# A decoder layer on one core: the first stage in another order

## The chip, the cores and the metric

The kernel runs on 1 core of a Trainium2 chip (trn2). The metric is device microseconds (us) of one execution; lower is better. The engines are PE (TensorE, matrix products), DVE (VectorE), ACT (ScalarE), POOL (GpSimd) and SP (SyncE, which only issues DMAs here). Each has its own instruction queue and runs it in order; they meet through semaphores.

## What is computed

One layer of a decoder with 1024 tokens of width 1024, all in fp32. The change touches only what happens before the attention rounds, so the reference is cut to that:

```python
n = _rmsnorm(h, g_mix[l])
proj = n @ w_in[l]
qa, ka, va, qb, kb, vb, gate_a, gate_b = jnp.split(proj, split_at, axis=-1)
qa = _partial_rope(heads(qa, N_HEADS_DIL), positions)
ka = _partial_rope(heads(ka, N_HEADS_DIL), positions)
o_a = merge(_dilated_attention(qa, ka, heads(va, N_HEADS_DIL)))
o_b = merge(_stick_breaking(heads(qb, N_HEADS_SB), heads(kb, N_HEADS_SB), heads(vb, N_HEADS_SB)))
...
h = h + _memory_attention(_rmsnorm(h, g_mem_q[l]), _rmsnorm(mem, g_mem_kv[l]), w_q_mem[l], w_kv_mem[l], w_o_mem[l])
```

The memory (256 tokens) has a norm of its own, and its keys and values are `_rmsnorm(mem) @ w_kv_mem`: four key heads and four value heads of 128. They are needed late, in the memory attention; the query, key and value of the first pair of A-heads are needed at once.

## The kernel before

**Tiles and passes.** Activations lie with the features on the 128 partitions, as eight blocks of 128 features by 1024 tokens. Every fp32 product is made of three products of rounded parts: `hi*hi`, `lo*hi` and `hi*lo`, where `hi` is the rounded number and `lo` the rest. A weight tile of 128 x 1024 is split into `w_hi` and `w_lo` by POOL (`split`, L455 for `w_hi` in two instructions, L460 for `w_lo` in four). There are two buffers of each, used in turn: POOL may start to split tile n when PE has begun tile n-1 (semaphore `w_begun`), and PE may begin tile n when it is split (`w_split`, `begin_tile`). SP loads the tiles in the order in which `weight_stream` has packed them. One tile of `w_in` against all tokens is 48 matmuls with 512 columns (two halves of three passes of eight); a tile of the memory's weights is 24 matmuls with 256 columns.

**The first stage.** The program begins with the eight tiles of the memory's weights, K0 to K3 (one key head each) and V0 to V3 (in pairs, each pair makes two blocks of the values), and then three tiles of `w_in`: QA, KA, VA, the query, key and value of the first pair of A-heads. On their way PE also makes the mean of the memory's squares (L570), turns the memory's norm factor into a column (L576), and makes the mean of x's squares (L583). ACT rounds x into `n_hi` (L979) and squares it (L983), block by block in turn; DVE makes the rest `n_lo` (L1468) and adds up the squares in `rms` (L1473). The norm of x isn't applied to `n_hi`: it multiplies the product when DVE reads it out of PSUM (`read_out`, L1506). The memory's keys go PE -> DVE (`k_f`, L1454) -> ACT (`km_out` hi, L962) -> DVE (`km_out` lo, L1457), the values PE -> ACT (L967) -> DVE (L1462); both are then stored to HBM by four DMAs that ACT issues (L1003, L1004).

**Rotation.** DVE makes the angles from the positions (L1436 to L1444, then L1485 to L1487), ACT their sine and cosine (L994, L996, with a table load ahead and one behind). When QA is read out, ACT issues four small DMAs that swap rows of it (`swap_dma`, L1011); DVE multiplies and adds (`rope`, L1520 to L1524), ACT rounds (L1016), DVE makes the rest (`lo_part`, L1513). Then the same for KA. VA is transposed by PE (L624) and rounded by ACT (L1020) and DVE (L1529).

**What follows.** Four rounds (`round_`, three in a loop and the last by itself), in which PE puts attention of one pair of heads between the passes of the next ten tiles (KB first); then the gated mix, the output product, memory attention, the feed-forward part and the last norm.

**Buffers.** The tensors of a stage lie in the same SBUF space as those of the stages before and after (`phase`); a store or a tile of the next stage may be written only when what lay there has been used. The eight PSUM banks are `ps[:, 0..7, :]`.

Of the kernel before, what the change touches and what calls it, by code (L numbers as in the profile page):

```python
# [17 lines left out]
ALU = mybir.AluOpType  # L18
ACT = mybir.ActivationFunctionType
# [147 lines left out]
HEAD_UNITS = 2 * HEAD_TILES  # L167

# [5 lines left out]
def build(nc, xT, memT, positions, gains, weights, ident_d, rope_d, bias_d, mask_d, outT):  # L174
    with ExitStack() as ctx:
# [26 lines left out]
        def phase(*tensors):  # L202
# [122 lines left out]
        gained = sem("gained")  # L325


        B_MIX = 2
# [37 lines left out]
        KEYS_AT = (4, 5, 7)  # L366
# [155 lines left out]
        def _(pe):  # L522
# [40 lines left out]
            pe.wait_ge(mg_lo_s, KT)  # L563
            for t in range(2 * MH):
                begin_tile(t + 1)
                if t == 1:
                    pe.wait_ge(msq, 1)
                    pe.wait_ge(summed, 1)
                    for k in range(KT):
                        ins = pe.matmul(ps[:, 7, 0:NM], mean_w[:], mem_sq[:, k, :], start=(k == 0), stop=(k == KT - 1))  # L570
                    ins.then_inc(mmean, 1)
                if t == MH:
                    pe.wait_ge(mrms, 1)
                    pe.wait_ge(ident_in, 16)
                    for mt in range(2):
                        ins = pe.transpose(ps[:, 1, blk(mt)], mem_r[:, blk(mt)], ident[:])  # L576
                    ins.then_inc(r_col_full, 1)
                if t == MH + 2:
                    pe.wait_ge(r_col_ready, 1)
                    pe.wait_ge(kv_lo_s, 2)  # L580
                    pe.wait_ge(summed, KT + 1)
                    for half in range(2):
                        pe.matmul(ps[:, half, :], mean_w[:], rms[:, blk(half, HALF)], start=True, stop=True  # L583
                                  ).then_inc(bank_full, 1)
                if t < MH:
                    lead, last = passes(ps[:, 2 + t, 0:NM], lambda k: (t % 2, k * P), lambda k: mg_hi[:, k, :],
                                        lambda k: mg_lo[:, k, :], (0, 1, 2), range(KT), True, True)
                    last.then_inc(kv_full, 1)
                else:
                    first = t % 2 == 0  # L590
                    for mt in range(2):
                        item = MH + (t - MH) // 2 * 2 + mt
                        n = 0
                        for a, w in ((mg_hi, w_hi), (mg_lo, w_hi), (mg_hi, w_lo)):
                            for k in range(KT // 2):
                                last = pe.matmul(ps[:, 2 + item % 6, 0:NM], a[:, k + (0 if first else KT // 2), blk(mt)],  # L596
                                                 w[:, t % 2, blk(k, NM)], start=(first and n == 0),
                                                 stop=(not first and n == 3 * KT // 2 - 1))
                                if mt == 0 and n == 0:
                                    lead = last  # L600
                                n += 1
# [3 lines left out]

            pe.wait_ge(nlo_ready, KT)

# [107 lines left out]
            for half in range(2):  # L715
                if half:
                    pe.wait_ge(vt_lo_s, half)
# [1344 lines left out]
```

## Time and profile before

| what | value |
|---|---|
| median of 3 runs | 1856.89 us (1855.19 to 1857.27) |
| profiled execution, its time | 1855.3 us |
| its span (first to last instruction) | 1853.3 us |
| PE busy in the span | 1729.2 us, 93% |
| DVE, ACT, POOL busy | 62%, 42%, 42% |
| chain that ended last, PE's share | 80% |
| mean granted TensorE clock | 0.972 |

The page cuts the span into 40 slices of 46.3 us; PE's digits there are 3, 7 and then mostly 9. "Busy" is the share of time in which an instruction of the engine ran; "idle before <- X" is how long the engine had nothing to run before a group of instructions, and which engine's instruction ended that wait.

### The profile page before, as it was taken

The numbers are of one execution on the slowest core, as the hardware profiler recorded it, in microseconds if no ns is written. First come the engines' busy times: TensorE is split into PE (matmuls) and PEld (weight loads), VectorE is DVE, ScalarE is ACT, GpSimd is POOL, SyncE is SP. The second block draws the span as 40 slices with busy tenths as digits, with TensorE's granted clock in tenths as the row PEclk, the third lists the DMA queues.
The fourth block names the chain that finished last, engine by engine and source line by source line (L and its number), as shares of the span: only waits on it lengthen the run. The fifth ranks groups of instructions, "written<-read, shape, count | busy, mean of one in ns | idle before, by whom it ended". The sixth has DMA issues, their size and how long they took to land.

```text
span 1853.3 us, 24985 instructions
## 1 busy us (share of the span) xinstructions
PE 1729.2 (93%) x8350; PEld 1398.7 (75%) x8350; DVE 1155.9 (62%) x1685; ACT 782.4 (42%) x1291; POOL 776.4 (42%) x894
## 2 busy tenths in 40 slices
PE   3799999999999999969999888999999999999996
PEld 3677777777777777758887766788888888788884
DVE  7446795689468846975444569745545445566667
ACT  4215773577358646753212334533433334200013
POOL 5733222232223221224454105665666656534445
PEclk8899999999999999979999889999999999999998
DMA  5311112101211211164212000131121221422222
GB/s 196 125 40 44 42 50 67 46 29 60 67 36 39 66 53 39 52 230 157 109 45 91 23 12 23 46 111 70 68 91 68 92 89 68 154 96 91 91 91 91
DMA packets 51711, 141.73 MB, mean 76 GB/s; under 512 B 6192, under 2 KB 14640, under 8 KB 51504
## 3 DMA queue, kind: packets, MB, share of 16 engines
q1 hardware_dynamic: 32256, 101.35, 15.6%
q10 hardware_dynamic: 19376, 39.33, 6.5%
q8 instruction: 48, 0.79, 0.2%
q14 instruction: 31, 0.25, 0.0%
HBM read 109.20 MB, written 30.41 MB: 75 GB/s over the span
## 4 chain that ended last, share of the span: by engine, by line
PE 80%; DVE 8%; issue 4%; ACT 3%; POOL 2%; DVEq 0%; ACTq 0%; DMA 0%; POOLq 0%
PE ps L537 46%; PE ps L856 21%; PE ps L683 4%; PE ps L646 3%; PE ps L660 3%; POOL w_lo L488 1%; DVE e_row L1599 1%; DVE pt L1629 1%; DVE e_row L1596 1%; DVE rows L1608 1%; PE ps L679 1%; DVE sum_a L1805 1%; DVE h L1962 0%; DVE n_lo L1811 0%; PE ps L596 0%
## 5 line engine op out<-in xcount | busy, mean ns | idle before, releaser
L455 POOL TENSOR_SCALAR w_hi<-w_stage 128x512 fp32r<-128x512 f32 x186 | 126.8, 700 | 868.2 <-issue 459.8
L460 POOL TENSOR_TENSOR w_lo<-w_stage,w_hi 128x256 fp32r<-128x256 f32 x372 | 342.9, 953 | 7.7
L537 PE MATMUL ps<-n_hi,w_hi 128*128 128x512 f32 x1184 | 329.4, 400 | 11.8 <-DVE n_lo L1549 7.0
L537 PE MATMUL ps<-n_lo,w_hi 128*128 128x512 f32 x1184 | 320.8, 392 | 0.0
L537 PE MATMUL ps<-n_hi,w_lo 128*128 128x512 f32 x1184 | 320.7, 392 | 0.0
L537 PEld LDWEIGHTS ps<-n_hi,w_hi 128*128 128x128 f32 x1184 | 222.1, 191 | 60.3 <-issue 12.0
L537 PEld LDWEIGHTS ps<-n_lo,w_hi 128*128 128x128 f32 x1184 | 220.8, 188 | 45.7 <-issue 0.2
L537 PEld LDWEIGHTS ps<-n_hi,w_lo 128*128 128x128 f32 x1184 | 219.9, 188 | 44.8
L488 POOL TENSOR_TENSOR w_lo<-w_stage,w_hi 128x256 fp32r<-128x256 f32 x176 | 164.7, 956 | 120.9 <-ACT w_hi L1259 120.9
L1699 DVE TENSOR_TENSOR h<-ps,h 128x512 f32<-128x512 f32 (+1 forms) x176 | 121.2, 690 | 123.3 <-PE ps L537 123.3
L1081 ACT ACTIVATE pt<-ps 128x256 fp32r<-128x256 f32 (+3 forms) x96 | 78.0, 813 | 133.9 <-PE ps L660 133.7
L1312 ACT ACTIVATE snap<-ps 128x512 f32<-128x512 f32 x88 | 52.6, 598 | 180.1 <-PE ps L856 180.0
L488 POOL TENSOR_TENSOR w_lo<-t_raw,w_hi 128x256 fp32r<-128x256 f32 x132 | 109.1, 847 | 43.7 <-ACT w_hi L1259 43.4
L1629 DVE TENSOR_TENSOR pt<-ps,pt 128x256 fp32r<-128x256 f32 (+3 forms) x96 | 91.9, 957 | 49.9 <-ACT pt L1081 45.9
L856 PE MATMUL ps<-left,w_hi 128*128 128x512 f32 x308 | 122.7, 398 | 0.0
L856 PE MATMUL ps<-n_hi,w_hi 128*128 128x512 f32 x352 | 115.5, 399 | 6.1 <-POOL w_lo L488 4.2
L856 PE MATMUL ps<-n_lo,w_hi 128*128 128x512 f32 x352 | 114.8, 397 | 2.6 <-DVE n_lo L1814 2.6
L856 PE MATMUL ps<-n_hi,w_lo 128*128 128x512 f32 x352 | 114.4, 396 | 0.0
L1506 DVE TENSOR_TENSOR raw<-ps,rms 128x512 f32<-128x512 f32 x80 | 54.8, 685 | 90.6 <-PE ps L537 90.6
L1364 ACT ACTIVATE n_hi<-n_lo 128x1024 fp32r<-128x1024 f32 x22 | 22.1, 1052 | 186.3 <-DMA n_lo<-hidden_scratch 186.3
L856 PEld LDWEIGHTS ps<-n_hi,w_hi 128*128 128x128 f32 x352 | 66.5, 190 | 23.9 <-POOL w_lo L488 5.1
L660 PE MATMUL ps<-ident,rows 128*128 128x128 f32 x576 | 81.8, 280 | 0.0
(236 smaller groups left out, 3027.3 us busy)
## 6 DMA issues: line engine op xcount, KB each, us to landing
w_stage<-weights_in SPq DMA_DIRECT2D x116, 512.0 KB, 3.4
w_stage<-weights_in SPq DMA_DIRECT2D x44, 256.0 KB, 2.6
hidden_scratch<-u_f SPq DMA_DIRECT2D x22, 512.0 KB, 5.7
n_lo<-hidden_scratch SPq DMA_DIRECT2D x22, 512.0 KB, 4.1
gates_scratch<-raw ACTq DMA_DIRECT2D x16, 512.0 KB, 2.8
o_scratch<-o_sum ACTq DMA_DIRECT2D x64, 64.0 KB, 2.1
n_lo<-o_scratch ACTq DMA_DIRECT2D x8, 512.0 KB, 3.9
g_a<-gates_scratch ACTq DMA_DIRECT2D x8, 512.0 KB, 3.7
```

Of the source, the lines that this page charges most:

```text
L455: ins = pool.tensor_scalar(w_hi[:, b, at], stage[:, b, at], 1.0, 1.0, ALU.mult, ALU.mult)
L460: ins = pool.tensor_tensor(w_lo[:, b, at], stage[:, b, at], w_hi[:, b, at].bitcast(F32), ALU.subtract)
L488: ins = pool.tensor_tensor(w_lo[:, b, at], right(name)[:, blk(part, 2 * P)], w_hi[:, b, at].bitcast(F32), ALU.subtract)
L537: ins = pe.matmul(bank, w[:, b, c:c + P], mv(k), start=(first and n == 0), stop=(last and n == total - 1))
L646: ins = pe.matmul(ps[:, 2 + h, 0:width(s)], a[hs, blk(qb)], b[hs, at], start=(n == 0), stop=(n == 2 and not diagonal))
L660: ins = pe.transpose(ps_t[:, h, n, :], rows[:, s % 4, h, blk(n)], ident[:])
L683: ins = pe.matmul(ps[:, r, blk(h, 2 * P)], v_of[m][:, c + kb, h, :, :].rearrange("p a d -> p (a d)"), pt[:, h, kb, :, :].rearrange("p a q ...
L856: ins = pe.matmul(ps[:, bank, :], w[:, b, c + k * P:c + (k + 1) * P], left(name, k)[p == 1], start=(opening and p == 0 and k == 0), stop=( ...
L1081: act.activation(pt[:, :, 0:n, 0, :], ps_t[:, :, 0:n, :], ACT.Copy).then_inc(pt_hi_s, 1)
L1506: dve.tensor_tensor(raw[:, RAW[name], blk(half, HALF)], ps[:, half, :], rms[:, blk(half, HALF)], ALU.mult).then_inc(bank_free, 1)
L1629: dve.tensor_tensor(pt[:, :, 0:n, 1, :], ps_t[:, :, 0:n, :], pt[:, :, 0:n, 0, :].bitcast(F32), ALU.subtract).then_inc(pt_lo_s, 1)
L1699: dve.tensor_tensor(hj, ps[:, bank + half, :], hj, ALU.add).then_inc(bank_free, 1)
```

## The change

The order of the first stage's tiles becomes K0, QA, K1, KA, K2, K3, V0, V1, V2, VA, V3 (`HEAD`); PE, the weight stream and the PSUM banks follow it. `memory_tile` and `head_tile` are the old loops, taken apart. The mean of the memory's squares no longer waits for the second tile; the mean of x's squares stands behind QA, in banks 6 and 7.

```diff
+HEAD = ("K0", "QA", "K1", "KA", "K2", "K3", "V0", "V1", "V2", "VA", "V3")
+HEAD_BANK = {"QA": 0, "KA": 2, "VA": 0}
+KV_BANK = (4, 5, 4, 5, 2, 3, 6, 7)
...
+                    if n >= 2:
+                        pe.wait_ge(kv_lo_s, n - 1)
...
+                    if n == 0:
+                        pe.wait_ge(bank_free, B_MIX + 4)
+                    if n == 2:
+                        pe.wait_ge(r_col_ready, 1)
...
+                    if name == "VA":
+                        pe.wait_ge(bank_free, B_MIX + half + 1)
...
+            memory_tile("K0")
+            pe.wait_ge(msq, 1)
+            pe.wait_ge(summed, 1)
+            for k in range(KT):
+                ins = pe.matmul(ps[:, 7, 0:NM], mean_w[:], mem_sq[:, k, :], start=(k == 0), stop=(k == KT - 1))
+            ins.then_inc(mmean, 1)
+            head_tile("QA", (0, 2, 1), ((nhi_ready, KT - 1), (nlo_ready, KT - 1)))
             pe.wait_ge(nlo_ready, KT)
+            pe.wait_ge(summed, KT + 1)
+            pe.wait_ge(mrms_raw, 1)
...
-            pe.wait_ge(kv_lo_s, 2 * MH)
+            pe.wait_ge(kv_lo_s, MH)
+            pe.wait_ge(bank_free, B_MIX + 6)
             for half in range(2):
-                if half:
-                    pe.wait_ge(vt_lo_s, half)
-                pe.wait_ge(bank_free, B_MIX + 6)
-                v_transposes(half, 5)
+                v_transposes(half, 4 + half)
+            pe.wait_ge(kv_lo_s, MH + 2)
```

On ACT all eight blocks of x are rounded first and then squared, and the norm factor (L955, L956) is made at once behind the squares. The four stores of the memory's keys and values move behind the rounding of VA, and the wait for them into the round:

```diff
                 act.activation(n_hi[:, k, :], x_f[:, k, :], ACT.Copy, scale=gain[:, G_MIX + k:G_MIX + k + 1]
                                ).then_inc(nhi_ready, 1)
+            for k in range(KT):
                 if k >= 2:
                     act.wait_ge(summed, k)
                 act.activation(sq0[:, k % 2, :], x_f[:, k, :], ACT.Square).then_inc(squared, 1)
...
+            kv_hi(0)
+            for n, name in enumerate(("QA", "KA")):
+                act.wait_ge(bank_free, B_MIX + 2 * n + 2)
+                swap_dma(n, n)
+                kv_hi(1 + n)
+                act.wait_ge(rope_done, n + 1)
+                round_hi(name)
+            for t in range(3, 2 * MH):
                 kv_hi(t)
...
-            act.wait_ge(kv_out, 64)
...
+                    if s == N_A - 2:
+                        act.wait_ge(kv_out, 64)
```

On DVE the eight rests of x come ahead of the sums; the first sum adds two squares and the clearing of `rms` goes; two of the three steps that reduce the angles, and what follows them, move behind the sums:

```diff
-            dve.memset(rms[:], 0.0)
...
+            reduce_by(turns[0])
...
+            dve.wait_ge(squared, 2)
+            dve.tensor_tensor(rms[:], sq0[:, 0, :], sq0[:, 1, :], ALU.add).then_inc(summed, 2)
...
+            reduce_by(turns[1])
+            dve.wait_ge(xmean_full, 2)
+            for half in range(2):
+                dve.tensor_scalar(rms[:, blk(half, HALF)], ps[:, 6 + half, :], EPS, None, ALU.add).then_inc(xmean_raw, 1)
+            reduce_by(turns[2])
...
+            kv_lo(1)
+            dve.wait_ge(sin_ready, 2)
             rope(0, 64, step)
-            read_out("KA", 1, B_MIX + 3)
+            read_out("KA", 0, B_MIX + 2, HEAD_BANK["KA"])
+            read_out("KA", 1, B_MIX + 3, HEAD_BANK["KA"])
             lo_part("QA", 1, B_MIX + 2)
+            kv_lo(2)
+            rope(1, 64, step)
```

The layout of the first stage's buffers is another one (`x_f`, `mem_f` and `mem_sq` lie higher, `vm_out` and `km_out` with other paddings); sizes and types are the same.

PE at the start of the program. Here `mg_hi` and `mg_lo` are the memory's parts, `mem_sq` its squares, `n_hi` and `n_lo` those of x. Before:

```order
L537 MATMUL ps<-mg_hi,w_hi 128x256 x8
L537 MATMUL ps<-mg_lo,w_hi 128x256 x8
L537 MATMUL ps<-mg_hi,w_lo 128x256 x8
L570 MATMUL ps<-mem_sq,mean_w 128x256 x8
L537 MATMUL ps<-mg_hi,w_hi 128x256 x8
```

The same place now:

```order
L540 MATMUL ps<-mg_hi,w_hi 128x256 x8
L540 MATMUL ps<-mg_lo,w_hi 128x256 x8
L540 MATMUL ps<-mg_hi,w_lo 128x256 x8
L615 MATMUL ps<-mem_sq,mean_w 128x256 x8
L540 MATMUL ps<-n_hi,w_hi 128x512 x8
L540 MATMUL ps<-n_hi,w_lo 128x512 x8
L540 MATMUL ps<-n_lo,w_hi 128x512 x8
```

Behind K0 and the mean of the memory's squares stood K1; now QA stands there, with the pass that needs `n_lo` last.

PE at the end of the stage, from the last pass of VA on; `raw` holds VA as read out, L588 is a tile of the memory's values. Before:

```order
L537 MATMUL ps<-n_hi,w_lo 128x512 x8
L624 MATMUL ps<-ident,raw 128x128 x8
L720 UNCONDITIONAL_BRANCH
L720 ISA
L646 MATMUL ps<-qk 128x128 x6
```

And now:

```order
L540 MATMUL ps<-n_hi,w_lo 128x512 x8
L588 MATMUL ps<-w_hi,mg_hi 128x256 x4
L588 MATMUL ps<-w_hi,mg_lo 128x256 x4
L588 MATMUL ps<-w_lo,mg_hi 128x256 x4
L588 MATMUL ps<-w_hi,mg_hi 128x256 x4
L588 MATMUL ps<-w_hi,mg_lo 128x256 x4
L588 MATMUL ps<-w_lo,mg_hi 128x256 x4
L654 MATMUL ps<-ident,raw 128x128 x8
```

Between VA's last pass and the transposes of VA stands the last value tile, V3.

DVE between the sums of the squares and the read-out of QA. `vm_out` are the memory's values, `k_f` and `km_out` its keys, `rms` the norm of x. Before:

```order
L1462 SCALAR_TENSOR_TENSOR vm_out<-ps,r_col,vm_out 128x256 x4
L1492 TENSOR_SCALAR rms<-ps 128x512 x2
L1494 MEMSET swap 128x1024
L1496 MEMSET o_sum 64x256 x2
L1498 MEMSET raw 128x1 x2
L1506 TENSOR_TENSOR raw<-ps,rms 128x512 x3
```

And now:

```order
L1510 TENSOR_SCALAR rms<-ps 128x512 x2
L1468 SCALAR_TENSOR_TENSOR ang<-rnd,ang 128x1024
L1512 TENSOR_SCALAR ang<-ang 128x1024
L1513 SCALAR_TENSOR_TENSOR rnd<-ang 128x1024
L1514 TENSOR_SCALAR rnd<-ang,rope_c 128x1024
L1515 TENSOR_SCALAR rnd<-rnd 128x1024
L1516 MEMSET swap 128x1024
L1518 MEMSET o_sum 64x256 x2
L1520 MEMSET raw 128x1 x2
L1481 TENSOR_TENSOR k_f<-ps,mem_r 128x256
L1484 TENSOR_TENSOR km_out<-k_f,km_out 128x256
L1529 TENSOR_TENSOR raw<-ps,rms 128x512 x2
```

The work on the angles and the first key of the memory now stand between the mean of x and the read-out of QA, and the values of the memory behind it.

## Rows read from the trace of the kernel before

**Rows 1.** Busy time by stretch: us; then busy us and instructions per engine; PEclk; DMA.

```profile
21.30:82.28 60.98, 39.94 (x215) 36.64 (x215) 34.92 (x35) 20.19 (x26) 47.29 (x48) 0.80 0.22 70
82.28:119.61 37.33, 35.04 (x159) 28.47 (x159) 16.05 (x21) 5.45 (x8) 13.05 (x18) 0.99 0.37 120
119.61:180.00 60.39, 60.39 (x309) 47.32 (x308) 29.81 (x77) 25.31 (x63) 18.08 (x24) 0.98 0.14 42
```

**Rows 2.** PE in order of time, first stage: start, duration, group, [idle before <- releaser].

```profile
30.00 5.29 PE L570 MATMUL ps<-mem_sq,mean_w 128*128 128x256 f32 x16 [3.35 <-POOL w_lo L460]
...
43.46 2.08 PE L537 MATMUL ps<-mg_hi,w_hi 128*128 128x256 f32 x8 [5.31 <-POOL w_lo L460]
...
65.02 1.22 PE L596 MATMUL ps<-w_hi,mg_hi 128*128 128x256 f32 x4 [3.21 <-POOL w_lo L460]
...
70.30 2.10 PE L583 MATMUL ps<-rms,mean_w 128*128 128x512 f32 x4
76.82 0.74 PE L596 MATMUL ps<-w_hi,mg_hi 128*128 128x256 f32 x4 [1.53 <-POOL w_lo L460]
...
82.28 2.08 PE L537 MATMUL ps<-n_hi,w_hi 128*128 128x512 f32 x8 [2.37 <-DVE rms L1492]
...
93.26 1.98 PE L537 MATMUL ps<-n_hi,w_hi 128*128 128x512 f32 x8
...
118.10 0.74 PE L624 MATMUL ps<-ident,raw 128*128 128x128 f32 x4 [1.41 <-DVE vA L1529]
118.77 0.90 PE L646 MATMUL ps<-qk 64*128 64x128 f32 x6
119.61 3.17 PE L537 MATMUL ps<-n_hi,w_hi 128*128 128x512 f32 x8
```

**Rows 3.** As rows 1: stretches from a start of PE to the clock's rise.

```profile
30.00:33.10 3.10, 3.10 (x7) 2.52 (x8) 0.00 (x0) 0.00 (x0) 0.00 (x0) 0.50 0.55 169
65.02:70.60 5.58, 5.58 (x25) 5.58 (x26) 0.97 (x2) 4.54 (x6) 4.01 (x6) 0.50 0.28 94
119.61:121.95 2.34, 2.34 (x8) 1.86 (x7) 1.56 (x6) 1.18 (x7) 1.31 (x3) 0.50 0.00 0
```

**Rows 4.** POOL in order of time: the splits of K2 and V2.

```profile
35.57 2.17 POOL L455 TENSOR_SCALAR w_hi<-w_stage 128x512 fp32r<-128x512 f32 x2 [5.62 <-PE ps L537]
37.82 5.59 POOL L460 TENSOR_TENSOR w_lo<-w_stage,w_hi 128x256 fp32r<-128x256 f32 x4
...
65.76 1.20 POOL L455 TENSOR_SCALAR w_hi<-w_stage 128x512 fp32r<-128x512 f32 x2 [0.80 <-PE ps L596]
67.05 2.81 POOL L460 TENSOR_TENSOR w_lo<-w_stage,w_hi 128x256 fp32r<-128x256 f32 x4
```

**Rows 5.** DVE, groups of 0 to 119.6 us: count, busy us, mean ns, idle before.

```profile
L1473 DVE TENSOR_TENSOR rms<-rms,sq 128x1024 f32<-128x1024 f32 x8 | 13.5, 1685 | 0.0
L1468 DVE SCALAR_TENSOR_TENSOR n_lo<-x_f,gain,n_hi 128x1024 fp32r<-128x1024 f32 x8 | 12.8, 1596 | 0.6 <-ACT n_hi L979 0.6
L1506 DVE TENSOR_TENSOR raw<-ps,rms 128x512 f32<-128x512 f32 x6 | 4.2, 692 | 19.2 <-PE ps L537 19.2
...
L1520 DVE TENSOR_TENSOR swap<-swap,sin_m 128x1024 f32<-128x1024 f32 x2 | 2.4, 1216 | 0.0
...
L1485 DVE SCALAR_TENSOR_TENSOR rnd<-ang 128x1024 f32<-128x1024 f32 x1 | 1.7, 1743 | 0.0
...
L1487 DVE TENSOR_SCALAR rnd<-rnd 128x1024 f32<-128x1024 f32 x1 | 1.2, 1206 | 0.0
```

**Rows 6.** ACT and its DMA queue in order of time, as rows 2.

```profile
15.18 1.15 ACT L979 ACTIVATE n_hi<-x_f,gain 128x1024 fp32r<-128x1024 f32 x1 [4.00 <-DMA x_f<-x_t_in]
...
64.46 1.28 ACT L994 ACT_TABLE_LOAD   x1 [4.29 <-DVE rnd L1486]
...
94.24 3.27 ACTq L1011 DMA_DIRECT2D swap<-raw  x4
```

**Rows 7.** DVE in order of time, the first product with the swapped rows.

```profile
99.51 1.22 DVE L1520 TENSOR_TENSOR swap<-swap,sin_m 128x1024 f32<-128x1024 f32 x1
```

More of the change, by code:

```diff
@@ L559, in mean, with memory_tile @@
                               stop=True).then_inc(mean_full, 1)
[L563 to L586, printed above, removed]
+            def memory_tile(name):
+                index, n = HEAD.index(name), int(name[1])
+                begin_tile(index + 1)
+                b = index % 2
+                if name[0] == "K":
+                    if n >= 2:
+                        pe.wait_ge(kv_lo_s, n - 1)
+                    lead, last = passes(ps[:, KV_BANK[n], 0:NM], lambda k: (b, k * P), lambda k: mg_hi[:, k, :],
                                         lambda k: mg_lo[:, k, :], (0, 1, 2), range(KT), True, True)
@@ L1476, in _ @@
                     dve.tensor_scalar(mem_r[:], ps[:, 7, 0:NM], EPS, None, ALU.add).then_inc(mrms_raw, 1)
[L1477 to L1484 removed]
+            pi = 3.1415925
+            reduce_by(turns[1])
+            dve.wait_ge(xmean_full, 2)
+            for half in range(2):
+                dve.tensor_scalar(rms[:, blk(half, HALF)], ps[:, 6 + half, :], EPS, None, ALU.add).then_inc(xmean_raw, 1)
+            reduce_by(turns[2])
+            step(dve.tensor_scalar(ang[:], ang[:], pi, -pi, ALU.min, ALU.max))
             step(dve.scalar_tensor_tensor(rnd[:, 1, :], ang[:], -1.0, ang[:], ALU.mult, ALU.max))
@@ L1487, in _ @@
             dve.tensor_scalar(rnd[:, 1, :], rnd[:, 1, :], -1.0, pi / 2, ALU.mult, ALU.add).then_inc(ang_ready, 1)
-            for t in range(len(KEYS_AT) + 1, 2 * MH):
-                kv_lo(t)
-            dve.wait_ge(bank_full, 2)
-            for half in range(2):
-                dve.tensor_scalar(rms[:, blk(half, HALF)], ps[:, half, :], EPS, None, ALU.add).then_inc(bank_free, 1)
-            dve.wait_ge(sin_ready, 2)
             step(dve.memset(swap[:], 0.0))
@@ L1987, in weight_stream @@
     w = tiles(w_in, P)
-    out = list(tiles(w_kv_mem[:, :MH * P], P))
+    head = {f"K{n}": t for n, t in enumerate(tiles(w_kv_mem[:, :MH * P], P))}
     values = w_kv_mem[:, MH * P:]
     first, second = (tiles(values[n:n + D // 2], NM) for n in (0, D // 2))
-    for f, g in zip(first, second):
-        out += [f, g]
+    for n, pair in enumerate(zip(first, second)):
+        head.update({f"V{2 * n + m}": t for m, t in enumerate(pair)})
     place = {"QA": 0, "KA": 4, "VA": 8, "QB": 12, "KB": 16, "VB": 20}
-    out += [w[place[n]] for n in ("QA", "KA", "VA")]
+    head.update({n: w[place[n]] for n in ("QA", "KA", "VA")})
+    out = [head[n] for n in HEAD]
     for i in range(PAIRS):
```

126 lines of the change are left out of this document (70 added, 56 removed).

## The prediction

> **What bounds the kernel now.** I read the busy times by stretch first, to see whether PE waits where the change is made [rows 1]. Behind 119.61 us, where the first attention round starts its first product (KB), PE is busy for all of 60.39 us: whatever brings the start of the rounds forward by a microsecond takes a microsecond off the end. Between 21.30 and 82.28 it is different: PE works for 39.94 of 60.98 us, at a mean granted clock of 0.80. In the third stretch of the stage (QA, KA, VA, to 119.61) it is busy for 35.04 of 37.33 us.
>
> The timeline of PE says what it waits for [rows 2]: before nearly each of the memory's tiles it stands idle (5.31 us before K2, 3.21 before V1, 1.53 before V3) and the releaser is POOL's `w_lo`. POOL may split tile n only while PE works on tile n-1, since there are two buffers. A tile of the memory holds PE for 3.1 us (V3, from 76.82 to 79.91, which is 2.37 before 82.28), but the split takes 4.10 us when DVE is quiet (65.76 to 69.86) and 7.84 when it is busy in SBUF (35.57 to 43.41) [rows 4]. So the stage's bound is the loop "PE begins, POOL splits, PE begins", about 0.8 us plus a split for a tile. A tile of `w_in` holds PE for 10.98 us (82.28 to 93.26, QA), long enough to hide any split behind it. Before, the three stand at the end, where one of them covers the split of the next, and the eight short tiles cover nothing.
>
> The clock goes with that: 0.50 for 3.10 us after the start at 30.00, for 5.58 after 65.02, and for 2.34 after KB's start [rows 3]. Half of each such stretch is lost.
>
> **The change, part by part.** I follow PE through the new order. K0 and all before it stay as they are; K0 ends at 26.65 (3.35 before 30.00). What is named a begin is PE's.
>
> Mean of the memory's squares. It no longer waits for the second split. It took 5.29 us, 3.10 of them at half clock; at full clock it takes 3.7. It comes directly behind 5.35 us of K0, so I take full clock: 26.65 to 30.4. At half clock until as late as before it would be 31.9.
>
> QA. Its split is the second, done at 30.0 before, where PE waited for it [rows 2], and its beginning and DVE's load beside it don't change, so 30.4 stands. It also needs x. ACT begins to round at 15.18, when the first block lands, and needs 1.15 each [rows 6]; done one behind the other, all are ready by about 25. DVE begins the rests at 16.3 instead of behind the angles: 8 x 1.60 = 12.8, to 29.1 [rows 5]. QA's last pass, which needs them, begins later than that. QA ends at 41.4.
>
> The sums of squares are seven of 1.69 instead of eight [rows 5], 11.8, plus 0.4 for the memory's factor and 1.1 of waiting for ACT's third square, since ACT's squares are now held by two buffers that DVE empties only after 29.1: to 42.4, or 41.5 if the last two run beside a quiet POOL at about 1.22, the mean of the product with the swapped rows, which also reads two SBUF tensors [rows 5]. That meets QA's end: nobody waits much. The mean of x, 2.1 [rows 2], and **K1 begins at 43.5**.
>
> KA. POOL begins 0.75 after K1 (65.02 to 65.76) [rows 2, 4]. DVE then reads two halves out of PSUM and has the angles: two of about 1.74 and three of about 1.21 [rows 5], 7.1 us in SBUF. This is the nearest to K2's split, so close to 7.84; the first 0.8 us is undisturbed, and I take 7.4 (bounds 4.1 and 7.84). KA begins at 51.7, after 5 us of idle, so at half clock: 3.10 to 5.58 us of it [rows 3] cost 1.6 to 2.8; I take 2.2. KA ends at 64.9, K2 begins.
>
> The five tiles between KA and VA. K2's 3 us of PE cover K3's split, and so on; each step is 0.8 plus the split. DVE's work beside them, at 1.2 an operation, decides: the end of QA's rotation and its rest for K3, KA's rotation and rest for V0, little for V1, V2 and VA. Going through DVE's list and counting POOL at half speed where they meet (which is 4.10 against 7.84), I get splits of 5.6, 6.8, 4.5, 4.1 and 4.1: K3 at 71.3, V0 78.9, V1 84.2, V2 89.1, and VA at 94.4 if one value tile at half clock adds 0.4. With all five at 4.1 it is 90, with all at 7.84 it is 108; the first three have DVE beside them for half of the time at most, so I keep 3 us either way.
>
> VA and what is behind it. 10.98, and 0.8 for a half-clock start (0 to 2.8; QA, begun after 2.37 idle, lost nothing) [rows 2]: 106.2. V3's split is hidden behind VA, V3 itself takes 3.1: 109.3. The transposes of VA are both issued at once into two banks; one group is 0.67 (118.10 to 118.77), so 1.3, to 110.6. They need VA's read-out (0.69 a half), which V3 hides. The first logits take 0.84 (118.77 to 119.61). **KB begins at 111.5.** Its split starts 0.75 behind V3's begin and takes 4.1: 111.1, just in time.
>
> Against that stands KB's begin before, 119.61, and the half-clock stretch of 2.34 behind it, which V3 right ahead should prevent: 1.2. The gain is 119.61 + 1.2 - 111.5 = **9.3 us**.
>
> Edits that I cost at nothing, with their cover. The clearing of `rms` lay before DVE had work. The chain of DVE and ACT behind the mean of x: norm factors, angles ready at about 51, two table loads of 1.28 and sine and cosine of about 1.1 [rows 6], QA read at 57.5, four swap issues of 3.27 on ACT's queue, landed at most 2.0 later (97.51 to 99.51) [rows 6, 7], three products of 1.22: QA turned at 66.6, KA read at 68.3, KA's rotation 76.7, r_col at 77. PE asks for KA's read-out at V0 (78.9), for r_col at V2 (89.1) and for `kv_lo` of K1 (62) at K3 (71.3): some 10 us of slack each. ACT's swap issues now hold up the rounding of K1 and K2 behind them, and through that DVE; this is inside the times given. The four stores move behind VA's rounding; like the swaps they hold ACT's queue for some 3.3 us, and what is queued behind them is the first exponential, whose sums DVE takes up only behind KB's first half (over 5 us). The wait for them inside the rounds comes some 100 us after. SP's loads keep their rhythm with the tiles; no DMA moves past another on its queue. The read-outs now follow waits for the memory's keys on DVE; that is in the chain above.
>
> The Trainium skill, in "SBUF — State Buffer" (section "Reading the diagram"), says that a DVE operation with two SBUF inputs and a POOL operation exclude each other for the whole instruction. By that rule each of POOL's six instructions would wait for a DVE operation, and KA's split would be nearer 10 than 7.4, for a gain near 7. The trace doesn't show a full block: POOL's split is 1.9 times as long, while DVE's rests take 1.60, so the sum goes by the rows.
>
> The sum is made against the profiled execution, 1855.3 us; its span is 1853.3, and the 2.0 around it stay. 1855.3 - 9.3 = 1846.0. The median of the runs shown is 1.6 above that execution, so I forecast **1847.5**. This kernel's measurement can tell about 0.2% (3.7 us) from no change.
>
> **The rivals.**
>
> *A, slower: the clock stays down.* The short tiles with waits between them keep PE at half clock, and KA and VA, which ran at full speed in one row before, run at half clock to their ends. Each takes 10.98 more, less the 2.2 and 0.8 that I have counted: 19 us, so 1866. For it: 0.50 through all of the 5.58 us behind 65.02 [rows 3]. Against it: every start there was back at full clock within 5.58 us of work, and KA and VA are twice as long. It would need 18 more microseconds at half clock than I counted to eat the gain. The skill's page "TensorE: Matmul & The Clock Gate" ("HAM oscillation — how this bites in real kernels") tells of a kernel that is slowed so at every tile by waits; by its rule this rival.
>
> *B, the DVE and ACT chain ends last.* QA and KA are now turned in the middle of the stage, and V0 waits for KA's read-out, K3 for K1's rest. If the swaps land late or ACT's queue delays a rounding, by 16 us in all instead of the 10 of slack, V0 begins 6 later and the gain is 3.5 to 5: 1852.
>
> *C, less meeting on SBUF.* If the splits of KA, K3 and V0 are nearer 4.1 than I have them (3.3, 1.5 and 2.7 less) and VA starts at full clock, the gain is 13 to 15: 1843.
>
> *D, the lead is lost in the round.* The stores and VA's rounding put ACT's first exponentials 3 to 5 us later against KB than before; if DVE's list then holds up KB's second half or the second logits, the lead goes into the first round: 1855 to 1857.
>
> **How the numbers follow.** My forecast 0.63 (gain 6 to 12.5), C 0.13, B 0.10, D 0.07, A 0.07. The range 1842.5 to 1854 leaves out A, D and the far end of C, less than 2 in 10; its lower end is a gain of 14, its upper end one of 3, which takes in the half-clock mean (1.5), KA's and VA's longest restarts (2.6) and 3 us in the middle tiles. Faster by over 0.2%: forecast, C and most of B, 0.85. Within: D and the rest of B, 0.08. Slower: A, 0.07.
>
> **What would show it.** In the trace after: QA begins near 30.4 with no wait behind the mean, K1 near 43.5, KA near 51.7 with POOL as releaser, VA near 94, KB near 111.5, and PE without a gap from VA on; the rounds as long as before. If PE waits at K3, V0 or V2 for DVE, it is B; if KA or VA show 22 us, it is A; if KB is early and the span not shorter, D. The prediction is wrong in its reason if the gain comes from elsewhere than these begins.

## The result, and the profile after

The changed kernel takes 1842.12 us (median of 4 runs, 1841.01 to 1843.35). The kernel before, run beside it, takes 1856.04 us (median of 4, 1855.18 to 1857.27). The ratio is 0.9925, with a 95% interval of 0.9907 to 0.9942: 13.9 us faster. The forecast was 1847.5 with a range of 1842.5 to 1854. Its direction was right, and the time lies 0.4 us below the lower end; two of the four runs lie inside the range.

| what | before | after |
|---|---|---|
| median | 1856.04 us | 1842.12 us |
| profiled execution, its time | 1855.3 us | 1843.35 us |
| its span | 1853.3 us | 1841.3 us |
| K0's begin on PE | 21.30 us | 19.95 us |
| KB's begin on PE | 119.61 us | 107.99 us |
| from KB's begin to the end of the span | 1733.7 us | 1733.3 us |

The head of the page after, and its line on the engines (busy us, share of the span, instructions):

```profile
span 1841.3 us, 24985 instructions
...
PE 1726.0 (94%) x8350; PEld 1396.0 (76%) x8350; DVE 1150.8 (62%) x1683; ACT 782.3 (42%) x1291; POOL 775.7 (42%) x894
```

The span is 12.0 us shorter, and 11.6 of them lie ahead of KB. Busy time by stretch of the kernel after, in the columns of [rows 1]: the stage from K0 to KB, the first part of the round, the mean of the memory's squares, and KA's start.

```profile
19.95:107.99 88.04, 72.61 (x373) 62.80 (x373) 50.77 (x56) 26.73 (x33) 61.55 (x66) 0.90 0.22 75
107.99:180.00 72.01, 72.01 (x379) 56.54 (x380) 38.38 (x98) 32.53 (x78) 22.11 (x30) 1.00 0.24 81
25.04:28.66 3.62, 3.62 (x18) 2.85 (x16) 3.62 (x3) 1.22 (x2) 3.62 (x3) 1.00 0.00 0
50.26:55.60 5.34, 5.34 (x13) 4.18 (x14) 4.31 (x11) 3.22 (x4) 4.19 (x6) 0.51 0.28 100
```

From K0 to KB the kernel before needed 98.31 us, of which PE worked for 74.98 (the first two lines of [rows 1] added up). Now it is 88.04, with 72.61 of work. So PE idles 15.4 us instead of 23.3, and 7.9 us of the gain are waits that are gone. It works 2.4 us less, with the same products to make; the mean granted clock goes with that, 0.90 over the stage against 0.87 before (the 0.80 and 0.99 of [rows 1], weighted by their lengths). K0 begins 1.35 earlier. Together this is the 11.6 us by which KB is early. Behind KB the granted clock is 1.00 at once, where it was 0.50 for 2.34 us [rows 3].

PE after, in order of time (start, duration, group, [idle before <- releaser]), with the begins that the prediction named:

```profile
19.95 2.05 PE L540 MATMUL ps<-mg_hi,w_hi 128*128 128x256 f32 x8 [19.95 <-POOL w_lo L463]
...
25.04 3.62 PE L615 MATMUL ps<-mem_sq,mean_w 128*128 128x256 f32 x16
29.64 2.14 PE L540 MATMUL ps<-n_hi,w_hi 128*128 128x512 f32 x8 [0.98 <-POOL w_lo L463]
...
50.26 3.78 PE L540 MATMUL ps<-n_hi,w_hi 128*128 128x512 f32 x8 [4.25 <-POOL w_lo L463]
53.84 2.79 PE L540 MATMUL ps<-n_lo,w_hi 128*128 128x512 f32 x8
...
69.29 2.08 PE L540 MATMUL ps<-mg_hi,w_hi 128*128 128x256 f32 x8 [2.30 <-POOL w_lo L463]
...
78.00 1.22 PE L588 MATMUL ps<-w_hi,mg_hi 128*128 128x256 f32 x4 [4.12 <-POOL w_lo L463]
...
92.34 2.08 PE L540 MATMUL ps<-n_hi,w_hi 128*128 128x512 f32 x8 [1.57 <-POOL w_lo L463]
...
103.33 0.63 PE L588 MATMUL ps<-w_hi,mg_hi 128*128 128x256 f32 x4
...
106.15 1.03 PE L654 MATMUL ps<-ident,raw 128*128 128x128 f32 x8
...
107.99 2.09 PE L540 MATMUL ps<-n_hi,w_hi 128*128 128x512 f32 x8 [0.32 <-POOL w_lo L463]
```

Every releaser here is POOL's `w_lo`; none is DVE or ACT. The loop of begin and split is still the stage's bound, with fewer turns in which nothing covers the split. One turn is PE's own: V0 runs at a mean clock of 0.53, takes 5.1 us (78.00 to 83.09), and V1 follows it without a wait.

### The profile page after: what moved, and what is told of

Same layout as the page of the kernel before. It is cut to its first block, busy times and chain, and to the rows that moved or that the text cites. A ratio compares the mean times of both kernels' runs of the same rounds, so it can differ in the third digit from the quotient of the medians.

```text
span 1841.3 us, 24985 instructions
## 1 busy us (share of the span) xinstructions
PE 1726.0 (94%) x8350; PEld 1396.0 (76%) x8350; DVE 1150.8 (62%) x1683; ACT 782.3 (42%) x1291; POOL 775.7 (42%) x894
## 3 DMA queue, kind: packets, MB, share of 16 engines
q1 hardware_dynamic: 32256, 101.35, 15.4%
## 4 chain that ended last, share of the span: by engine, by line
PE 79%; DVE 8%; issue 4%; ACT 3%; POOL 1%; DVEq 0%; ACTq 0%; DMA 0%; POOLq 0%
PE ps L540 45%; PE ps L881 22%; PE ps L713 4%; PE ps L676 3%; PE ps L690 3%; POOL w_lo L491 1%; DVE e_row L1634 1%; DVE pt L1664 1%; DVE e_row L1631 1%; DVE rows L1643 1%; PE ps L709 1%; DVE sum_a L1840 1%; DVE h L1997 0%; DVE n_lo L1846 0%; ACT p_m L1250 0%
```

## The experiments

All ratios are to the kernel before, run beside each on the same chip. Its median was 1856.09 us in the first batch, 1855.73 in the second and 1856.59 in the third.

### The pair again: is K0's early begin part of the change?

K0 began 1.35 us earlier, where I had said that all before it stays as it is. Both kernels ran once more, unchanged: the theory was that this lead repeats, the rival that it was a chance of one start.

> The changed kernel once more, for a closer interval and a second profile. The forecast was a gain of 9.3 us; four executions gave a median gain of 13.9, the profiled pair 12.0. Theory 1 (the stage's own terms were smaller than I summed): KB's begin is again near 108.0, the gain 12 to 14. Theory 2 (K0's begin at 19.95 instead of 21.30 is chance of that execution, since the first weights landed 0.84 us earlier): K0 begins near 21 here, KB near 109, the gain 11 to 12.

> The kernel before once more, for a second profile. Theory 1 (the earlier begin of K0 belongs to the change, as DVE is quieter beside POOL's first split): K0 begins at 21.3 again, KB at 119.6. Theory 2 (chance): K0 begins anywhere between 20.0 and 21.5, with the landing of the first weights.

Measured: 1841.86 us (median of 5, 1839.75 to 1843.21), ratio 0.9919 (0.9904 to 0.9934), and 1857.74 for the one run of before. K0 began at 19.69 and at 21.25. In all eleven profiles of kernels with the new stage it lies between 18.93 and 20.11. So the lead belongs to the change, but not all of it in this pair. POOL begins the first split when the first weights land, and how long the split takes comes on top. Before:

```profile
12.75 2.28 POOL L455 TENSOR_SCALAR w_hi<-w_stage 128x512 fp32r<-128x512 f32 x2 [12.30 <-DMA w_stage<-weights_in]
15.12 6.04 POOL L460 TENSOR_TENSOR w_lo<-w_stage,w_hi 128x256 fp32r<-128x256 f32 x4
```

And after, first POOL, then DVE beside it:

```profile
11.91 2.12 POOL L458 TENSOR_SCALAR w_hi<-w_stage 128x512 fp32r<-128x512 f32 x2 [11.46 <-DMA w_stage<-weights_in]
14.12 5.69 POOL L463 TENSOR_TENSOR w_lo<-w_stage,w_hi 128x256 fp32r<-128x256 f32 x4
```

```profile
15.59 2.95 DVE L1495 SCALAR_TENSOR_TENSOR n_lo<-x_f,gain,n_hi 128x1024 fp32r<-128x1024 f32 x2 [0.48 <-ACT n_hi L1004]
19.20 9.81 DVE L1495 SCALAR_TENSOR_TENSOR n_lo<-x_f,gain,n_hi 128x1024 fp32r<-128x1024 f32 x6 [0.66 <-ACT n_hi L1004]
```

Of the 1.35 us, 0.84 are an earlier landing (11.91 instead of 12.75), and 0.5 are a shorter split (7.9 us instead of 8.4). In the second pair the landing gives 0.4 and the split 1.1. The landing differs between executions of all these kernels: POOL begins at 12.50 and 12.75 in the two profiles of before, and between 11.88 and 12.93 in the eleven of the new stage. The split separates them: 8.4 and 8.6 us before, 6.1 to 7.9 in all eleven. Before, DVE worked without a gap beside it (the angles until 18.9, then rest and sum of x); now it has `n_lo`, which it can only make as fast as ACT rounds, and it stands idle for 0.48 and 0.66 us. The two shortest splits, 6.1 and 6.3, are those of two runs below in which DVE stood idle for longer there (1.89 us, and 0.96 and 0.51). That goes with the shorter split; no run took this one cause away by itself.

The second profile of before also shows how much one execution differs from another. PE in it:

```profile
29.95 6.44 PE L570 MATMUL ps<-mem_sq,mean_w 128*128 128x256 f32 x16 [3.83 <-POOL w_lo L460]
...
82.78 3.34 PE L537 MATMUL ps<-n_hi,w_hi 128*128 128x512 f32 x8 [2.37 <-DVE rms L1492]
```

The mean took 6.44 us instead of the 5.29 of [rows 2], and QA's first pass 3.34 instead of 2.08, behind the very same wait of 2.37. KB began at 121.64 there. The execution from which I predicted was 2 us quicker in this stage than its repetition; between the two second profiles KB is early by 13.9.

### One part undone at a time

The theory was that three parts of the change each hold some of the gain: the mean that no longer waits for a split, the last value tile behind VA, and x rounded ahead of its squares. The rival was that the interleaving of large and small tiles does the work and the rest trims it. First, the mean waits for the second split again:

```diff
             memory_tile("K0")
+            begin_tile(2)
             pe.wait_ge(msq, 1)
```

> In the changed kernel the mean of the memory's squares waits for the second split again, as in the kernel before. By my chain the second split ends at 29.6 and the mean's 3.6 us (up to 5.3 at half clock after 4.6 us idle) then lie ahead of QA: KB and the end 3.6 to 5.3 us later than in the changed kernel, some 1846 to 1847.5 us. Rival (the sums of squares, not QA, release the mean of x): the sums end at 41 anyway and half of it is hidden, 0 to 2 us later.

Measured: 1846.30 us (4 runs, 1846.1 to 1847.41), ratio 0.9946 (0.9930 to 0.9963). PE:

```profile
29.28 6.45 PE L616 MATMUL ps<-mem_sq,mean_w 128*128 128x256 f32 x16 [4.37 <-POOL w_lo L463]
```

The same sixteen products take 6.45 us behind a wait of 4.37, against 3.62 directly behind K0. QA begins at 35.38 instead of 29.40 (the second profile of after), KB at 111.99 instead of 107.77: 4.2 us, and 4.4 in the median. This part is worth 4 us, inside the 3.6 to 5.3 that were expected. QA itself begins 6.0 later; most of the rest comes back at V0 (81.89 instead of 77.81), whose split takes 6.9 us there and 7.9 in the changed kernel.

Then V3 ahead of VA:

```diff
-HEAD = ("K0", "QA", "K1", "KA", "K2", "K3", "V0", "V1", "V2", "VA", "V3")
+HEAD = ("K0", "QA", "K1", "KA", "K2", "K3", "V0", "V1", "V2", "V3", "VA")
...
-            for name in ("K3", "V0", "V1", "V2"):
+            for name in ("K3", "V0", "V1", "V2", "V3"):
                 memory_tile(name)
             head_tile("VA")
-            memory_tile("V3")
```

On DVE all rests of the memory's values stand ahead of VA's read-out to match.

> In the changed kernel V3 goes ahead of VA, so VA is the last tile as it was before. By my chain V3's split no longer hides behind VA (+4.7), V3's 2.8 us are gone from behind VA, VA's read-out (0.7) now lies ahead of the transposes, and PE may drop to half clock before KB (up to 1.2): KB and the end 2.4 to 3.8 us later than in the changed kernel, 1844.5 to 1846. Rival (the place of V3 does nothing, since KB's split then hides better): within 0.5 us.

Measured: 1846.42 us (4 runs, 1845.09 to 1847.8), ratio 0.9948 (0.9932 to 0.9965). PE at the stage's end:

```profile
108.07 1.06 PE L653 MATMUL ps<-ident,raw 128*128 128x128 f32 x8 [0.88 <-DVE raw L1528]
...
109.54 2.11 PE L540 MATMUL ps<-n_hi,w_hi 128*128 128x512 f32 x8
```

The transposes now wait 0.88 for the read-out that V3 had hidden, and V3's own split is no longer covered. KB is 1.8 us late in this profile, and its span 2.2 longer, while the median is 4.6 up. The scatter of single executions accounts for the rest: this profiled execution was 1.3 below its median, that of the changed kernel 1.1 above its own. So the direction is shown, and the size lies somewhere between 2 and 4.6 us.

Then x rounded and squared in turn, as before, on ACT and on DVE. The memory's factor is taken up two blocks later, since its mean isn't ready at the third:

```diff
                                ).then_inc(nhi_ready, 1)
-            for k in range(KT):
                 if k >= 2:
                     act.wait_ge(summed, k)
...
-                if k == 2:
+                if k == 4:
                     dve.wait_ge(mmean, 1)
```

> In the changed kernel x is rounded and squared block by block in turn again, on ACT, and DVE makes rest and sum in turn (the memory's factor behind the fifth sum, so that DVE doesn't stand waiting for it). DVE's work is the same in sum, the sums end near 41 as now, but the last rests of x are there near 39 instead of 29. By my chain QA's last pass then waits: QA ends near 44.8 instead of 40.7, the end is 3.5 to 4.5 us later than in the changed kernel, about 1846. Rival (QA's last pass is released early enough because the rests run ahead of the passes): within 1 us.

Measured: 1845.83 us (4 runs, 1844.11 to 1847.58), ratio 0.9949 (0.9932 to 0.9965). PE:

```profile
33.22 3.75 PE L540 MATMUL ps<-n_hi,w_hi 128*128 128x512 f32 x8 [5.13 <-ACT n_hi L1004]
36.77 2.77 PE L540 MATMUL ps<-n_hi,w_lo 128*128 128x512 f32 x8
```

And ACT, with the memory's norm factor (`mem_r`) and, 0.77 behind its begin, the rounding that QA waits for:

```profile
31.18 0.42 ACT L1011 ACTIVATE mem_r<-mem_r 128x256 f32<-128x256 f32 x1 [2.08 <-DVE mem_r L1506]
...
31.95 1.13 ACT L1004 ACTIVATE n_hi<-x_f,gain 128x1024 fp32r<-128x1024 f32 x1
```

The size came, but by luck, since it came at another place than I had expected. I had looked at `n_lo`, which QA's last pass needs; PE waits for the seventh `n_hi`, which its first pass needs. ACT may write its third square only when DVE has made the first sum (two squares), so ACT waits for DVE's pairs of rest and sum: 1.26 us ahead of the third square and 0.51 ahead of the sixth. The longest wait, 2.08, is for the memory's factor, which in ACT's queue stands behind the sixth square and so, in this run, ahead of the seventh rounding. QA begins 3.8 us late, and at half clock: 3.75 and 2.77 us for passes that otherwise take 2.14 and 1.99. To round first isn't only to have the rests earlier; it takes ACT's roundings out of DVE's pace and puts them ahead of the memory's factor. How much of the loss would stay with the factor behind the last rounding was not run.

Then all three together, which leaves of the change the new order as far as V2, the rotation in the middle of the stage and the late stores:

> The changed kernel with three parts undone together: the mean of the memory's squares behind the second split, x rounded and squared in turn, V3 ahead of VA. What is left is QA and KA between the memory's tiles. Each alone cost about 4 us (4.4, 4.0, 4.6). Theory (the first two hold up the same thing, QA's end, so only the later one counts): KB begins near 114, 6 to 9 us later than in the changed kernel, 1848 to 1851; QA and KA between the tiles are then worth the remaining 5 to 8 us against the kernel before. Rival (they add): 13 us later, 1854 to 1855, and the interleaving alone would be worth about 1.

Measured: 1856.09 us (10 runs, 1854.42 to 1857.69), ratio 0.9998 (0.9989 to 1.0008). The theory of this run, that a good part of the gain would stay, fell; the losses add, as the rival said, and the time is a little above its 1854 to 1855. The three losses in the ratio (0.0027, 0.0029 and 0.0030 against 0.9919) add up to 0.0086, and together they cost 0.0079. In KB's begin they are 4.2, 1.8 and 4.5 us apart, 10.4, and 10.2 together (117.92). What is left of the change gains nothing that the times can tell: the interval reaches from 2.0 us faster to 1.5 slower. In the traces KB is 1.7 and 3.7 us earlier than in the two profiles of before. QA in this run, on DVE, then ACT, then PE:

```profile
34.56 0.42 DVE L1506 TENSOR_SCALAR mem_r<-ps 128x256 f32<-128x256 f32 x1 [3.30 <-PE ps L616]
```

```profile
35.02 0.42 ACT L1011 ACTIVATE mem_r<-mem_r 128x256 f32<-128x256 f32 x1 [5.47 <-DVE mem_r L1506]
```

```profile
37.06 2.40 PE L540 MATMUL ps<-n_hi,w_hi 128*128 128x512 f32 x8 [2.54 <-ACT n_hi L1004]
```

A late mean holds DVE for 3.30 us, DVE's `mem_r` holds ACT for 5.47, and behind it in ACT's queue stand the last roundings of x that QA waits for. Before, K1 stood in QA's place and needed none of it. So with QA as the second tile, and the memory's factor where it stands in ACT's queue, the early mean and the early rounding are necessary, not merely useful. With the factor behind all roundings QA might need neither as much; that was not run.

### Rival D: the wait for the stores

Rival D of the prediction was that stores and late exponentials on ACT cost the lead at the start of the round. Here ACT waits for their landing at once, as it did before, and not deep in the round:

```diff
+            act.wait_ge(kv_out, 64)
...
-                    if s == N_A - 2:
-                        act.wait_ge(kv_out, 64)
```

> The changed kernel, but ACT waits for the four stores of the memory's keys and values right behind them, as in the kernel before, and not in the round. Theory (the first round's start has room on ACT): the first exponentials go from 111 to some 117, DVE's reciprocal behind KB's first half waits 2 us, PE doesn't: within 1 us of the changed kernel (1841 to 1843). Rival D (the round's start is short of ACT): 3 to 6 us later.

Measured: 1842.62 us (4 runs, 1841.26 to 1843.85), ratio 0.9929 (0.9912 to 0.9945), no different from the changed kernel. ACT, then DVE, at the start of the round:

```profile
114.66 0.31 ACT L1165 ACTIVATE mask_r<-mask_B 128x128 fp32r<-128x128 f32 x1 [7.87 <-DMA memory_kv_scratch<-vm_out]
```

```profile
116.18 0.17 DVE L1624 RECIPROCAL stat<-stat 128x2 f32<-128x2 f32 x1 [1.85 <-ACT rows L1068]
```

ACT's first exponential goes from 110.94 to 115.28, and DVE waits 1.85 us for it in front of one reciprocal; PE waits for neither. So PE didn't feel a delay of 4 us on ACT at that place. The two intervals overlap, and the 3 to 6 us that rival D asked for aren't there.

### What still lengthens the splits: DVE's work moved elsewhere

If DVE beside POOL sets the length of a split, DVE's work can be put beside QA, KA and VA, where a long split is hidden. First, the last reduction of the angles and what follows it, from the split of KA to behind QA's read-out (on ACT sine and cosine go behind QA's swaps, which isn't shown):

```diff
-            reduce_by(turns[2])
-            step(dve.tensor_scalar(ang[:], ang[:], pi, -pi, ALU.min, ALU.max))
...
             read_out("QA", 1, B_MIX + 1)
+            reduce_by(turns[2])
+            step(dve.tensor_scalar(ang[:], ang[:], pi, -pi, ALU.min, ALU.max))
...
             kv_lo(1)
```

> In the changed kernel the last four steps of the angles (DVE) and sine and cosine (ACT) move behind QA's read-out, out of KA's split. Theory (DVE's work in SBUF beside POOL's split is what KA waits for): KA's split 4.1 to 4.6 us instead of 6.7, KA begins near 48 instead of 50.3 after some 2 us of idle instead of 4.3, and perhaps at full clock: the end 2 to 5 us earlier than in the changed kernel, 1837 to 1840. Rival B (DVE's and ACT's chain is the bound): the chain gets longer by some 5 us and V0 or K3 waits for DVE: no gain, or up to 3 us later.

Measured: 1839.11 us (4 runs, 1837.74 to 1839.71), ratio 0.9910 (0.9894 to 0.9927). The split of KA in the changed kernel, and that of V0 for the next step:

```profile
43.41 1.21 POOL L458 TENSOR_SCALAR w_hi<-w_stage 128x512 fp32r<-128x512 f32 x2 [4.74 <-issue]
44.69 5.51 POOL L463 TENSOR_TENSOR w_lo<-w_stage,w_hi 128x256 fp32r<-128x256 f32 x4
...
70.03 3.12 POOL L458 TENSOR_SCALAR w_hi<-w_stage 128x512 fp32r<-128x512 f32 x2 [0.80 <-PE ps L540]
73.24 4.70 POOL L463 TENSOR_TENSOR w_lo<-w_stage,w_hi 128x256 fp32r<-128x256 f32 x4
```

With the angles moved, the splits of KA and of K3:

```profile
43.05 1.21 POOL L458 TENSOR_SCALAR w_hi<-w_stage 128x512 fp32r<-128x512 f32 x2 [4.74 <-issue]
44.34 2.81 POOL L463 TENSOR_TENSOR w_lo<-w_stage,w_hi 128x256 fp32r<-128x256 f32 x4
...
58.66 3.14 POOL L458 TENSOR_SCALAR w_hi<-w_stage 128x512 fp32r<-128x512 f32 x2 [3.94 <-issue]
61.88 4.67 POOL L463 TENSOR_TENSOR w_lo<-w_stage,w_hi 128x256 fp32r<-128x256 f32 x4
```

And PE, where KA and K3 begin:

```profile
47.21 2.11 PE L540 MATMUL ps<-n_hi,w_hi 128*128 128x512 f32 x8 [1.56 <-POOL w_lo L463]
...
66.59 2.07 PE L540 MATMUL ps<-mg_hi,w_hi 128*128 128x256 f32 x8 [5.11 <-POOL w_lo L463]
```

KA's `w_lo` goes from 5.51 to 2.81 us, and two things follow at once: KA begins 2.8 us earlier than in the second profile of after, and behind 1.56 us of idle instead of 4.25 it starts at full clock, 2.11 us for the pass that took 3.78. But QA's rotation doesn't move with it; it now falls on K3's split, which goes from 5.06 to 7.89, and PE waits 5.11 there. KB begins at 104.71, 3.1 us earlier.

Second, KA's rotation and both rests (`lo_part`) between and behind the two read-outs of VA, where there is time (on ACT the rounding of KA moves to match):

```diff
-            lo_part("QA", 1, B_MIX + 2)
             kv_lo(2)
-            rope(1, 64, step)
...
-            lo_part("KA", 2, B_MIX + 4)
...
             read_out("VA", 0, B_MIX + 4)
+            lo_part("QA", 1, B_MIX + 2)
+            rope(1, 64, step)
             read_out("VA", 1, B_MIX + 5)
+            lo_part("KA", 2, B_MIX + 4)
```

> In the changed kernel QA's rest and KA's rotation on DVE move behind the read-out of VA's first half, out of K3's and V0's splits. Theory (contention sets these splits): V0's split 4.1 instead of 7.9 us, K3's 4.3 instead of 5.0: V0 begins 4 us earlier, the end 3.5 to 4.5 us earlier than in the changed kernel, about 1838. Rival (the rotation now ends too late for the first logits): the first logits wait, gain below 2 us or a loss.

Measured: 1840.12 us (4 runs, 1837.47 to 1841.22), ratio 0.9910 (0.9894 to 0.9927). V0's split on POOL, then PE at V0 and at KB:

```profile
68.86 1.38 POOL L458 TENSOR_SCALAR w_hi<-w_stage 128x512 fp32r<-128x512 f32 x2 [0.60 <-PE ps L540]
70.33 2.79 POOL L463 TENSOR_TENSOR w_lo<-w_stage,w_hi 128x256 fp32r<-128x256 f32 x4
```

```profile
73.17 0.73 PE L588 MATMUL ps<-w_hi,mg_hi 128*128 128x256 f32 x4 [1.72 <-POOL w_lo L463]
...
103.71 1.65 PE L540 MATMUL ps<-n_hi,w_hi 128*128 128x512 f32 x6 [1.15 <-POOL w_lo L463]
```

The 7.9 us of V0's split are 4.3 now, and V0 begins 4.6 us earlier than in the second profile of after. KB begins at 103.71, 4.1 earlier, after a wait of 1.15, since the rest of KA meets its split. Of this only 1.7 us are left between the medians. The profiled execution itself, at 1841.22, was the slowest of its four: the code behind KB, which does the same work, took 1735.5 us in it, the longest of all profiles.

Both together:

> Both moves: angles behind QA's read-out, QA's rest and KA's rotation behind VA's first half. If the two are independent, as the loop of splits has it, the gains add: 6 to 9 us earlier than the changed kernel, 1833 to 1836. Rival (the chain of DVE and ACT has become the bound): less than the larger of the two.

Measured: 1836.96 us (4 runs, 1835.88 to 1837.41), ratio 0.9896 (0.9879 to 0.9912), KB at 101.21. They gain 4.9 us, less than expected, and 6.6 in KB's begin. QA's rotation is still beside K3's split. So in the last one the memory's second key is put behind that rotation, which can then begin as soon as ACT has the cosine:

```diff
-            kv_lo(1)
             dve.wait_ge(sin_ready, 2)
             rope(0, 64, step)
+            kv_lo(1)
```

> Both moves of the run with angles and KA's rotation late, and the rest of K1's key behind QA's rotation, so that QA's rotation starts when sine and cosine are ready and not behind ACT's rounding of K1: QA's rotation some 2 us earlier and mostly off K3's split, which was 6.7 us there. Theory (contention sets K3's split): K3 begins 1 to 1.5 us earlier and the end as much, some 1835.5. Rival: K3 now waits for K1's rest: no gain.

Measured: 1835.04 us (4 runs, 1833.74 to 1835.29), ratio 0.9883 (0.9867 to 0.9900), KB at 100.32. K3's split without the last edit, and with it:

```profile
58.81 3.11 POOL L458 TENSOR_SCALAR w_hi<-w_stage 128x512 fp32r<-128x512 f32 x2 [3.95 <-issue]
62.01 3.62 POOL L463 TENSOR_TENSOR w_lo<-w_stage,w_hi 128x256 fp32r<-128x256 f32 x4
```

```profile
59.16 2.26 POOL L458 TENSOR_SCALAR w_hi<-w_stage 128x512 fp32r<-128x512 f32 x2 [3.94 <-issue]
61.50 2.96 POOL L463 TENSOR_TENSOR w_lo<-w_stage,w_hi 128x256 fp32r<-128x256 f32 x4
```

This version computes the whole layer and is the fastest of all: 7 us below the changed kernel, whose interval of the ratio (0.9904 to 0.9934) lies clear of its own, and 21.5 below the kernel before. In KB's begin the last edit is worth 0.9 us. The single steps on the way (0.9910, 0.9910, 0.9896) overlap with their neighbours; for them it is the begins in the traces that carry the verdict.

## Why the prediction was right, and where not

The mechanism held. PE waits for POOL's split, the large tiles cover it, and the stage's end moves the program's end: KB is 11.6 us early, and the span is 12.0 shorter. Against the forecast's begins:

| begin | forecast, us | after, us | change of the difference |
|---|---|---|---|
| mean of the memory's squares | 26.65 | 25.04 | -1.6 |
| QA | 30.4 | 29.64 | +0.8 |
| K1 | 43.5 | 42.57 | -0.2 |
| KA | 51.7 | 50.26 | -0.5 |
| K2 | 64.9 | 63.73 | +0.3 |
| K3 | 71.3 | 69.29 | -0.8 |
| V0 | 78.9 | 78.00 | +1.1 |
| V1, V2, VA | 84.2, 89.1, 94.4 | 83.09, 87.66, 92.34 | -1.2 |
| V3 | 106.2 | 103.33 | -0.8 |
| transposes, logits, KB | 109.3, 110.6, 111.5 | 106.15, 107.12, 107.99 | -0.6 |

Step by step:

- **Mean of the squares: right.** No wait, full clock, 3.62 us against the 3.7 that I took. With the wait back it costs 4 us.
- **"K0 and all before it stay as they are": wrong**, by 1.35 us. I put a change there at nothing because I followed PE, and forgot the loop that I had just described: DVE's work beside the first split had changed. The split was 0.5 us shorter in this pair and 1.1 in the second; the other 0.84 of this pair are the first weights' earlier landing, which differs from execution to execution. K0 ended 1.6 early. Half of that came back at the second split, which now runs beside a DVE without a gap (before, DVE was done 1.3 us ahead of its end): from 19.77 to 29.58, 9.8 us, where it took 8.8 before.
- **The three disturbed splits: wrong one by one, right in their sum by luck.** I took 7.4, 5.6 and 6.8 us for KA, K3 and V0; they are 6.8, 5.1 and 7.9, 19.8 in either case. KA's rotation met V0's split and not half of it, as I had counted. The steps from QA to V0 are off by 0.1 together. The Trainium skill's rule in "SBUF — State Buffer" (section "Reading the diagram"), by which the two engines exclude each other for a whole instruction, gave by my estimate some 10 us for KA's split; the trace shows 6.8, so here neither was shut out for as long as that.
- **KA's half-clock start: right.** The granted clock is 0.51 for 5.34 us, and KA holds PE for 13.47 us (50.26 to 63.73) instead of 10.98: 2.5, where I had 2.2.
- **The value tiles and VA: too dear by 2 us.** I allowed half-clock starts of 0.4 and 0.8 and counted 0.8 from PE's begin to POOL's. The releases took 0.4 to 0.7. V0 did begin at half clock and set its own step, 5.1 us where I had 5.3; V1 and V2 held the loop for 4.6 and 4.7 us, and VA began at full clock behind 1.57 us of idle (2.08 for its first pass).
- **The end of the stage: too dear by 0.6.** The transposes run as one group of 1.03 and the logits follow 0.97 behind their start, where I had put 1.3. PE isn't quite without a gap there: it waits 0.32 for KB's split, which I had put just in time.
- **KB's own restart: gone, but its 1.2 us can't be found.** The granted clock is 1.00 from KB on. Yet the code behind KB takes 1733.3 us after 1733.7 before, and between 1730.0 and 1735.5 over all thirteen profiles, though its work is the same. A term of 1.2 is below what one profile can tell there.
- **Rivals.** A, the clock that stays down, wasn't seen: KA is back at full clock within 5.34 us, and QA and VA start at it. The short tiles do lose clock behind their waits: K3's first pass takes 2.08 us behind 2.30 of idle where K2's takes 1.12, and V0's begins with 1.22 behind 4.12 where V3's takes 0.63. The Trainium skill's page "TensorE: Matmul & The Clock Gate" (section "HAM oscillation — how this bites in real kernels") describes a kernel that loses the clock again at each tile; this trace shows that for KA, K3 and V0, but not for QA and VA, and nowhere to the end of a long tile. B wasn't seen either: no wait of PE there is put down to DVE or ACT; such waits came only in runs that undo a part. D is refuted by the run above. C comes closest to the measured time (1843); of its two conditions one held, VA's start at full clock, and the other did not: the splits that it made short were not short in their sum.

So the mechanism was right, and the step that failed is the size of the sum: KB at 111.5, where it began at 107.99, 3.5 us earlier. Three terms make it up. "K0 and all before it stay as they are" was put at nothing: K0 ended 1.6 early, and 0.8 of that was left at QA. The value tiles and VA were taken 2.0 too dear: releases that I counted at 0.8 took 0.4 to 0.7, and VA, for which I had added 0.8, began at full clock. The end of the stage was 0.6 shorter. From QA to V0 the errors cancel to 0.1. Against that, of the 1.2 that I had put behind KB only 0.4 shows, which leaves 2.7 us between the expected and the profiled execution (1846.0 and 1843.35). The other 2.7 are a second step that failed, the one from one execution to the median. I added 1.5, because before's profiled execution was quicker than the median of its runs. After's profiled execution was the slowest of its four, 1.2 above the median. I had carried over a property of one execution as if it were one of the kernel.

The range followed from that. Its lower end left room for a gain of 14 against an execution whose stage was 2 us quicker than that of its repetition. Several small terms of the same sign were not in it; I had asked only which large one could fail. By how little it was missed, 0.4 us, is less than the four runs differ among themselves.

## What to carry to other kernels

Where a double-buffered preparation bounds a stage, count what the other engines do beside each single preparation, the first one included, and put their work beside the long consumers that hide it: here that gave another 7 us. Before a long tile is put early, look at what it needs through every queue, since an order that alone gained nothing that the times could tell gained 14 us with two operands made ready for it and a tile moved behind. When most terms of a sum are taken on the careful side, the sum is biased, and the range has to be shifted to the other side.

## What I had not expected of the hardware

- The same wait of 2.37 us ahead of QA in the kernel before led to a first pass of 2.08 us in one execution and of 3.34 in another. Waits of 1.5 to 1.6 us (ahead of VA, and of KA with the angles moved) were followed by 2.08 to 2.14, and waits of 4.24 to 4.25 (ahead of KA) by 3.47 to 3.78.
- DVE's clearing of tensors didn't lengthen POOL's split. With the angles moved, DVE beside KA's split, which took 4.1 us as in [rows 4] beside a quiet DVE:

```profile
44.34 0.91 DVE L1511 MEMSET swap<- 128x1024 f32 x1 [0.16 <-issue]
45.43 0.55 DVE L1513 MEMSET o_sum<- 64x256 f32 x2 [0.18 <-DVE swap L1511]
```

- The same work behind KB took 1730.0 to 1735.5 us over the thirteen profiles: 5.5 us, 0.3%, two fifths of the gain in question.
